# Second feed-forward block with its normalised input stored in reverse token order and read backwards by TensorE

## The chip, the cores and the metric

One Trainium2 chip, one of its cores. The metric is the device time of one execution in microseconds; of several executions the median is given. Operands of the large products are float32r, TensorE's reduced-precision float32, in high and low parts.

## What is computed

A trunk of two layers on 512 tokens of width 1024. Each layer has a mixer block and then a SwiGLU feed-forward block of hidden width 2816, both on an RMS-normalised input and added to the residual. The change touches the feed-forward block of the second layer:

```python
def rmsnorm(x, g):
    y = x * lax.rsqrt(jnp.mean(x * x, axis=-1, keepdims=True) + EPS)
    return y * g

for layer in range(2):
    x = x + mixer(layer, rmsnorm(x, mix_norm[layer]))     # two kinds of mixers
    h = rmsnorm(x, ffn_norm[layer])
    gate, up = jnp.split(h @ w_ffn_in[layer], 2, axis=-1)
    x = x + (jax.nn.silu(gate) * up) @ w_ffn_out[layer]
```

## The kernel before

**Layout.** The residual is held transposed, `xT`: 128 partitions (features), 8 feature tiles, 512 tokens along each partition. The input of each block is `xT` times the norm's gain; the factor of each token (`row_scale`, from the sum of squares) is applied after the projection. That input is kept in two parts of float32r, `h_hi` (ScalarE, `h_high`, L727: a copy that rounds to float32r) and `h_lo` (VectorE, `h_low`, L1146: xT times gain minus h_hi). There are four such rounds: `rnd` 0 and 2 before the mixers, 1 and 3 before the feed-forward blocks. Tiles are [128, 8, 512], so one feature tile of one part is 2 KB of consecutive memory in a partition.

**Products.** `product` (L1683 to L1685) makes three matmuls for each product of a weight tile and an input tile: high by high, high by low, low by high. The weights are the stationary operand (128 x 128), the 512 tokens the moving one, a PSUM bank of 512 float32 the result. The profile's names give the moving operand first in these groups: `ps<-h_hi,w_hi`.

**Weights.** The queue of SyncE brings 188 loads of up to 128 x 1024 float32 into two raw slots; ScalarE makes `w_hi` (L697), VectorE `w_lo` (L1122), in a ring of four slots. A slot is free when TensorE has read it (`load_used`). The order of all this is written out by hand in each engine's program; the steps of the feed-forward blocks are in a loop of five turns with two groups each.

**The second block's input projection** (`ffn_in(1, 0)`, rnd = 3) has 11 groups of 256 hidden columns, gate and up. A group takes 4 loads (`half_group`), each with 4 feature tiles and 2 banks. The first two loads of a group use the feature tiles 0 to 3, the other two 4 to 7. So the first group can start when the first four feature tiles of h are there, while VectorE still adds the second half of the mixer's output to `xT`. Between its second and third load stands the `mean` (L1716), a matmul of the matrix of ones with the sums of squares `acc`. ScalarE and VectorE make `row_scale` from it (L746, L751, L1181, L1187). Each group's result is taken out of PSUM by VectorE (L1406 gate times row_scale, L1410 up times silu), with ScalarE (L883 silu, L886 high part) and GpSimd (L581) between.

VectorE's order around the start of the block: `add_x` adds four banks to `xT` (L1382), and between these the operations of h_lo (L1146) and of the sum of squares (L1157, L1160) of the tile before; ScalarE makes h_hi (L727) and the squares (L735) as each `xT` tile comes.

The mixers, the first block and the output projections read h, where they do, with the same helper `H`, in token order.

Of the kernel before, what the change touches and what calls it, by code (L numbers as in the profile page):

```python
# [16 lines left out]
F32 = mybir.dt.float32  # L17
# [3 lines left out]
ACT = mybir.ActivationFunctionType  # L21
# [91 lines left out]
def program(nc, x, mix_norm, ffn_norm, w_ffn_in, w_ffn_out, e_w_in, e_conv, e_q_gain, e_k_gain,  # L113
# [11 lines left out]
    def sb(name, shape, dt=F32, size=4):  # L125
        n = size
        for d in shape[1:]:
            n *= d
        t = at(name, shape, dt, place[0])
        place[0] += (n + 63) // 64 * 64  # L130
        return t


    xT = sb("xT", [P, DT, S])
    h_at = place[0]
    h_hi = sb("h_hi", [P, DT, S], F32R)
    h_lo = sb("h_lo", [P, DT, S], F32R)
# [84 lines left out]
    ps = ctx.enter_context(nc.psum_tensor("ps", [P, 8, S], F32))  # L222

    def sem(name):
        return ctx.enter_context(nc.semaphore(name))
# [26 lines left out]
    h_hi_ready = sem("h_hi_ready")  # L252
# [278 lines left out]
    def g_col(i, a=0, b=P):  # L531
        return gains[a:b, i:i + 1]
# [117 lines left out]
    def h_gain(rnd, ft):  # L650
        return mix0_gain[:, ft:ft + 1] if rnd == 0 else g_col({1: G_FFN0, 2: G_MIX1, 3: G_FFN1}[rnd] + ft)

    X_BANKS = (4, 5, 6, 7, 4, 5, 6, 7)
    V_BANKS = ((0, 2), (3, 3))

# [21 lines left out]
    def _(act):  # L677
# [41 lines left out]
        def h_high_first(ft):  # L719

            act.wait_ge(x_turned, ft + 1)
            act.activation(h_hi[:, ft, :], ps[:, X_BANKS[ft], :], ACT.Copy, scale=h_gain(0, ft)).then_inc(h_hi_ready, 1)

        def h_high(rnd, ft):

            act.wait_ge(x_ready, 8 * rnd + ft + 1)
            act.activation(h_hi[:, ft, :], xT[:, ft, :], ACT.Copy, scale=h_gain(rnd, ft)).then_inc(h_hi_ready, 1)  # L727

        def h_square(rnd, ft):
            f = 8 * rnd + ft  # L730
# [6 lines left out]
        def fin(rnd, ft):  # L737
            h_high(rnd, ft)
            h_square(rnd, ft)
# [371 lines left out]
    def _(dve):  # L1111
        TT, STT, TS, TC = dve.tensor_tensor, dve.scalar_tensor_tensor, dve.tensor_scalar, dve.tensor_copy
# [25 lines left out]
        def fin(rnd, ft):  # L1138

            h_low(rnd, ft)  # L1140
            h_sum(rnd, ft)

        def h_low(rnd, ft):
            f = 8 * rnd + ft
            dve.wait_ge(h_hi_ready, f + 1)
            STT(out=h_lo[:, ft, :], in0=xT[:, ft, :] if rnd else ps[:, X_BANKS[ft], :], scalar=h_gain(rnd, ft), in1=h_hi[:, ft, :].bitcast(F32),  # L1146
                op0=ALU.mult, op1=ALU.subtract).then_inc(h_lo_ready, 1)

        def h_sum(rnd, ft):
# [63 lines left out]
        def x_copy(ft):  # L1213
            dve.wait_ge(x_turned, ft + 1)
            TC(xT[:, ft, :], ps[:, X_BANKS[ft], :]).then_inc(x_ready, 1)

        for ft in range(0, DT, 2):
            h_low(0, ft)
            if ft == 0:
                dve.wait_ge(first_high, 1)  # L1220
                low_slice(E_Q, 0).then_inc(first_low, 1)
            h_low(0, ft + 1)
            if ft == 0:
                dve.wait_ge(hi_done, E_Q + 1)
                low_slice(E_Q, 1).then_inc(lo_done, 1)
                nxt[0] = 1
            x_copy(ft)
            x_copy(ft + 1)
            through(-3 + ft // 2)
            h_sum(0, ft)  # L1230
            h_sum(0, ft + 1)
# [320 lines left out]
        for j in range(4):  # L1552
            STT(out=yc[:, j, :].rearrange("p (n i) -> p n i", n=QT), in0=ps[:, j, :].rearrange("p (n i) -> p n i", n=QT),
                scalar=g_col(G_V + j), in1=gate_bias[:, j:j + 1, :].broadcast_to([P, QT, P]),
# [123 lines left out]
    def _(pe):  # L1678
        MM = pe.matmul

        def product(dst, st_hi, st_lo, mv_hi, mv_lo, start, stop):

            MM(dst, st_hi, mv_hi, start=start, stop=False)  # L1683
            MM(dst, st_hi, mv_lo, start=False, stop=False)  # L1684
            return MM(dst, st_lo, mv_hi, start=False, stop=stop)  # L1685

        def ready(n, shift=0):
            pe.wait_ge(lo_done, n + 1 + shift)

        def load(n, tiles, ks, moving, banks, first, last, shift=0, extra=None, before=None):  # L1690

            ready(n, shift)
            hi_, lo_ = w_hi[:, n % W_SLOTS, :], w_lo[:, n % W_SLOTS, :]
            for kk, k in enumerate(ks):
                if kk and extra:
                    extra()
                mh, ml = moving(k)
                th, tl = tiles(hi_, kk), tiles(lo_, kk)  # L1700
                for t, b in enumerate(banks):
                    if before:
                        before(kk, t)
                    ins = product(ps[0:P, b, :], th[t], tl[t], mh, ml,
                                  first and kk == 0, last and kk == len(ks) - 1)
            ins.then_inc(load_used, 1)

        def plain(cols, count):

            return lambda w, kk: [w[:, cols * kk + P * t:cols * kk + P * t + P] for t in range(count)]  # L1710

        H = lambda k: (h_hi[:, k, :], h_lo[:, k, :])

        def mean(m, bank, weights, src):

            MM(ps[:, bank, :], weights, src, start=True, stop=True).then_inc(sums_ready, 1)  # L1716
# [25 lines left out]
        def turn_x(quarter):  # L1742

            pe.wait_ge(x_loaded[quarter], 16)
            for ft in (2 * quarter, 2 * quarter + 1):
                if ft >= 4:
                    pe.wait_ge(x_ready, ft - 3)
                for t in range(QT):
                    ins = pe.transpose(ps[:, X_BANKS[ft], t * P:(t + 1) * P], x_tok[:, t, ft * P:(ft + 1) * P], ident)
                ins.then_inc(x_turned, 1)  # L1750
# [36 lines left out]
        for ft, arrived in ((0, x_first), (1, x_loaded[0])):  # L1787
            pe.wait_ge(arrived, 16)
            for t in range(QT):
                ins = pe.transpose(ps[:, X_BANKS[ft], t * P:(t + 1) * P], x_tok[:, t, ft * P:(ft + 1) * P], ident)  # L1790
            ins.then_inc(x_turned, 1)
# [145 lines left out]
        def ffn_in(layer, bank0):  # L1937

            n0, n1, c = FFN_IN[layer], FFN_OUT[layer], 22 * layer
            rnd = 1 + 2 * layer  # L1940

            def half_group(n, j, b0, shift):

                load(n + j, plain(256, 2), range(4 * (j // 2), 4 * (j // 2) + 4), H,
                     (b0 + 2 * (j % 2), b0 + 2 * (j % 2) + 1), j < 2, j >= 2, shift)

            pe.wait_ge(x_ready, 8 * rnd + 4)
            for j in range(4):
                if j in (0, 2):
                    pe.wait_ge(h_lo_ready, 8 * rnd + 2 * j + 4)  # L1950
                half_group(n0, j, 4 * bank0, 0)
                if j == 1:
                    pe.wait_ge(x_ready, 8 * rnd + 8)
                    pe.wait_ge(h_summed, 8 * rnd + 8)
                    mean(M_FFN0 if layer == 0 else M_FFN1, (1 - bank0) * 4, ones, acc[:, :])
            pe.wait_ge(rs_step, (M_FFN0 if layer == 0 else M_FFN1) + 1)
            with pe.Fori(0, NG_FF // 2) as i:
                for g in (1, 2):

                    pe.wait_ge(hidden_ready, 1 + c + 2 * (g - 1) + 4 * i)  # L1960
                    for j in range(4):
                        half_group(n0 + 4 * g, j, 4 * ((bank0 + g) % 2), 8 * i)
# [67 lines left out]
        for j in range(4):  # L2030
            n = O_CV + j
# [293 lines left out]
```

## Time and profile before

| | |
|---|---|
| median of 3 timed runs | 1114.03 us (1114.01 to 1114.13) |
| span of the profiled execution, first to last instruction | 1112.0 us |
| mean granted TensorE clock | 1.000 |
| TensorE busy (matmuls) | 1102.9 us, 5105 instructions |
| VectorE, ScalarE, GpSimd busy | 560.2, 420.4, 102.9 us |
| first matmul of the second block's input projection | 748.99 us |
| first matmul of its output projection | 989.26 us |

The profile has the span of one execution; the timed runs are whole executions, about 2 us longer. Busy time of TensorE (PE) contains matmuls that overlap each other, so the distance between starts says more than the duration of one. PEld are the loads of the stationary operand. An instruction of plain float32 matmul is two records in the trace.

### The profile page before, as it was taken

What the parts mean: (1) busy time and instruction counts of PE and PEld (TensorE: products, weight loads), DVE (VectorE), ACT (ScalarE), POOL (GpSimd) and SP (SyncE); (2) the same over time, 40 slices, a digit from 0 to 9 for tenths busy, and PEclk for the clock granted to TensorE, in tenths of its full rate; (3) what the DMA queues carried; (4) which work ended last, traced back from release to release, by engine and by line L of the source; (5) the groups of instructions that cost most, each with busy time, mean ns of one, the idle gap of its engine ahead of it and who ended that gap; (6) DMA issues with size and microseconds to landing.
All of it is one profiled execution on the core that took longest, in us unless ns stands there. A gap on an engine that the chain in (4) does not pass through costs nothing. (4 is left out here: it accounts for less than half of the span.)

```text
span 1112.0 us, 13661 instructions
## 1 busy us (share of the span) xinstructions
PE 1102.9 (99%) x5105; PEld 887.1 (80%) x5105; DVE 560.2 (50%) x784; ACT 420.4 (38%) x662; POOL 102.9 (9%) x126
## 2 busy tenths in 40 slices
PE   8999999999999999999999999999999999999998
PEld 7777788888888888888877766788888888888887
DVE  6678977434433433242466588656433433453321
ACT  5545445333322322231345567544322322332110
POOL 6000000001000100000002023000000100110000
PEclk9999999999999999999999999999999999999999
DMA  7422223333333233322233200223233333327431
GB/s 236 159 57 76 76 75 96 114 95 95 94 94 94 94 102 103 98 95 85 67 103 94 77 35 1 77 96 112 89 101 94 94 97 100 102 78 170 113 123 48
DMA packets 101289, 106.00 MB, mean 95 GB/s; under 512 B 26235, under 2 KB 77888, under 8 KB 101120
## 3 DMA queue, kind: packets, MB, share of 16 engines
q1 hardware_dynamic: 83536, 103.04, 29.8%
q10 hardware_dynamic: 16656, 2.10, 1.1%
q8 instruction: 27, 0.44, 0.2%
q0 software_dynamic: 1056, 0.30, 0.1%
q14 instruction: 14, 0.11, 0.0%
HBM read 101.23 MB, written 2.10 MB: 93 GB/s over the span
## 5 line engine op out<-in xcount | busy, mean ns | idle before, releaser
L1122 DVE TENSOR_TENSOR w_lo<-raw,w_hi 128x1024 fp32r<-128x1024 f32 (+2 forms) x192 | 224.6, 1176 | 419.1 <-ACT w_hi L697 416.3
L697 ACT ACTIVATE w_hi<-raw 128x1024 fp32r<-128x1024 f32 (+2 forms) x192 | 194.2, 1017 | 468.7 <-PE ps L1685 438.4
L1683 PE MATMUL ps<-h_hi,w_hi 128*128 128x512 f32 x912 | 359.7, 394 | 1.0 <-DVE h_lo L1146 1.0
L1685 PE MATMUL ps<-h_hi,w_lo 128*128 128x512 f32 x912 | 355.1, 389 | 0.0
L1684 PE MATMUL ps<-h_lo,w_hi 128*128 128x512 f32 x912 | 355.0, 389 | 0.0
L1683 PEld LDWEIGHTS ps<-h_hi,w_hi 128*128 128x128 f32 x912 | 171.3, 188 | 42.9 <-issue 6.7
L1684 PEld LDWEIGHTS ps<-h_lo,w_hi 128*128 128x128 f32 x912 | 171.2, 188 | 36.7 <-issue 1.7
L1685 PEld LDWEIGHTS ps<-h_hi,w_lo 128*128 128x128 f32 x912 | 171.2, 188 | 35.9
L581 POOL TENSOR_TENSOR ffn_t<-ffn_t,row_scale 128x512 f32<-128x512 f32 x40 | 51.0, 1295 | 614.2 <-ACT ffn_t L883 614.2
L1684 PE MATMUL ps<-w_lo,act_hi 128*128 128x512 f32 (+1 forms) x178 | 68.8, 387 | 0.0
L1685 PE MATMUL ps<-w_hi,act_lo 128*128 128x512 f32 (+1 forms) x178 | 68.8, 387 | 0.0
L1683 PE MATMUL ps<-w_hi,act_hi 128*128 128x512 f32 (+1 forms) x178 | 68.8, 387 | 0.0
L1683 PE MATMUL ps<-act_hi,w_hi 128*128 (+1 forms) x176 | 68.5, 389 | 0.0
L1684 PE MATMUL ps<-act_lo,w_hi 128*128 (+1 forms) x176 | 68.5, 389 | 0.0
L1685 PE MATMUL ps<-act_hi,w_lo 128*128 (+1 forms) x176 | 68.5, 389 | 0.0
L1410 DVE TENSOR_TENSOR ffn_t<-ps,ffn_t 128x512 f32<-128x512 f32 x44 | 30.4, 692 | 44.8 <-POOL ffn_t L581 40.7
L886 ACT ACTIVATE act_hi<-ffn_t 128x512 f32 (+1 forms) x44 | 27.8, 633 | 49.3 <-DVE ffn_t L1410 49.3
L883 ACT ACTIVATE ffn_t<-ffn_t 128x512 f32<-128x512 f32 x44 | 27.1, 632 | 39.0 <-DVE ffn_t L1406 39.0
L1683 PEld LDWEIGHTS ps<-w_hi,act_hi 128*128 128x128 f32 x178 | 33.4, 188 | 6.9
L1684 PEld LDWEIGHTS ps<-w_lo,act_hi 128*128 128x128 f32 x178 | 33.4, 188 | 6.8
L1685 PEld LDWEIGHTS ps<-w_hi,act_lo 128*128 128x128 f32 x178 | 33.4, 188 | 6.7
L1683 PEld LDWEIGHTS ps<-act_hi,w_hi 128*128 128x128 f32 x176 | 33.0, 188 | 6.9
(283 smaller groups left out, 1173.4 us busy)
## 6 DMA issues: line engine op xcount, KB each, us to landing
raw<-in_w_ffn_in SPq DMA_DIRECT2D x88, 512.0 KB, 3.5
raw<-in_w_ffn_out SPq DMA_DIRECT2D x44, 512.0 KB, 3.7
raw<-in_e_w_in SPq DMA_DIRECT2D x17, 512.0 KB, 3.7
raw<-in_o_w_in SPq DMA_DIRECT2D x8, 512.0 KB, 3.6
raw<-in_o_w_out SPq DMA_DIRECT2D x8, 512.0 KB, 3.6
raw<-in_e_w_out SPq DMA_DIRECT2D x8, 256.0 KB, 3.9
raw<-in_e_w_out SPq DMA_DIRECT2D x4, 512.0 KB, 4.5
out_tok<-x_blocks ACTq DMA_DIRECT2D x16, 128.0 KB, 2.5
```

Of the source, the lines that this page charges most:

```text
L581: pool.tensor_tensor(ffn_t[:, t, :], ffn_t[:, t, :], row_scale[:, :], ALU.mult).then_inc(silu_scaled, 1)
L697: ins = act.activation(dst, src, ACT.Copy)
L883: act.activation(ffn_t[:, b, :], ffn_t[:, b, :], ACT.Silu).then_inc(silu_done, 1)
L886: act.activation(dst[:, t, :], ffn_t[:, (t0 + t) % 4, :], ACT.Copy).then_inc(hidden_hi, 1)
L1122: ins = TT(dst, src, high, ALU.subtract)
L1410: TT(ffn_t[:, b, :], ps[:, b0 + 2 + t, :], ffn_t[:, b, :], ALU.mult).then_inc(hidden_ready, 1)
L1683: MM(dst, st_hi, mv_hi, start=start, stop=False)
L1684: MM(dst, st_hi, mv_lo, start=False, stop=False)
L1685: return MM(dst, st_lo, mv_hi, start=False, stop=stop)
```

## The change

In round 3, and only there, h_hi and h_lo are written through a view with the token axis reversed, and all that reads them uses the same view: VectorE, which subtracts h_hi, and TensorE, whose moving operand starts at the last address of the 2 KB and goes down by one element a column. The columns come out in token order.

```diff
+    def h_order(tile, rnd, ft):
+
+        return tile[:, ft, ::-1] if rnd == 3 else tile[:, ft, :]
+
...
         def h_high(rnd, ft):
 
             act.wait_ge(x_ready, 8 * rnd + ft + 1)
-            act.activation(h_hi[:, ft, :], xT[:, ft, :], ACT.Copy, scale=h_gain(rnd, ft)).then_inc(h_hi_ready, 1)
+            act.activation(h_order(h_hi, rnd, ft), xT[:, ft, :], ACT.Copy, scale=h_gain(rnd, ft)).then_inc(h_hi_ready, 1)
...
             dve.wait_ge(h_hi_ready, f + 1)
-            STT(out=h_lo[:, ft, :], in0=xT[:, ft, :] if rnd else ps[:, X_BANKS[ft], :], scalar=h_gain(rnd, ft), in1=h_hi[:, ft, :].bitcast(F32),
+            STT(out=h_order(h_lo, rnd, ft), in0=xT[:, ft, :] if rnd else ps[:, X_BANKS[ft], :], scalar=h_gain(rnd, ft),
+                in1=h_order(h_hi, rnd, ft).bitcast(F32),
                 op0=ALU.mult, op1=ALU.subtract).then_inc(h_lo_ready, 1)
...
             def half_group(n, j, b0, shift):
 
-                load(n + j, plain(256, 2), range(4 * (j // 2), 4 * (j // 2) + 4), H,
+                load(n + j, plain(256, 2), range(4 * (j // 2), 4 * (j // 2) + 4),
+                     lambda k: (h_order(h_hi, rnd, k), h_order(h_lo, rnd, k)),
                      (b0 + 2 * (j % 2), b0 + 2 * (j % 2) + 1), j < 2, j >= 2, shift)
```

## Rows read from the trace of the kernel before

**Rows 1.** The page: span, busy time, TensorE's slices and granted clock.

```profile
span 1112.0 us, 13661 instructions
...
PE 1102.9 (99%) x5105; PEld 887.1 (80%) x5105; DVE 560.2 (50%) x784; ACT 420.4 (38%) x662; POOL 102.9 (9%) x126
...
PE   8999999999999999999999999999999999999998
...
PEclk9999999999999999999999999999999999999999
```

**Rows 2.** Windows: busy us (instructions) of PE, PEld, DVE, ACT, POOL; clock; DMA.

```profile
745.00:775.00 30.00, 30.00 (x132) 24.48 (x131) 19.69 (x27) 15.22 (x21) 0.00 (x0) 1.00 0.28 88
...
185.36:424.80 239.44, 239.44 (x1056) 197.91 (x1055) 100.68 (x118) 77.80 (x95) 25.47 (x20) 1.00 0.31 97
```

**Rows 3.** Timeline of TensorE, both ends of the second block's input projection: start, us.

```profile
748.99 0.39 PE L1683 MATMUL ps<-h_hi,w_hi 128*128 128x512 f32 x1
...
759.87 1.02 PE L1716 MATMUL ps<-acc,small 128*128 128x512 f32 x2
760.33 0.80 PE L1683 MATMUL ps<-h_hi,w_hi 128*128 128x512 f32 x1
...
989.03 0.39 PE L1685 MATMUL ps<-h_hi,w_lo 128*128 128x512 f32 x1
989.26 0.39 PE L1683 MATMUL ps<-w_hi,act_hi 128*128 128x512 f32 x1
```

**Rows 4.** The chain that ended last, around the mean: start, us, what.

```profile
760.03 0.86 PE ps L1716 x2
760.89 0.23 PE ps L1683
```

**Rows 5.** Waits from 757 to 992 us: us in total, times, longest.

```profile
ACT w_hi L697 <- PE ps L1685: 119.5, 33, 4.5
DVE w_lo L1122 <- ACT w_hi L697: 113.9, 34, 4.3
```

**Rows 6.** Timeline of TensorE, first and last of 21 matmuls of 256 columns.

```profile
655.55 0.28 PE L1683 MATMUL ps<-w_hi,ckv_hi 128*128 128x256 f32 x1
...
657.95 0.28 PE L1685 MATMUL ps<-w_hi,ckv_lo 128*128 128x256 f32 x1
```

**Rows 7.** Tile h_hi from 749 us on: ns min/median/max, first and last start.

```profile
L1683 PE MATMUL ps<-h_hi,w_hi x352: 387/389/799, 749.0 to 988.6; 128*128 128x512 f32 x176
L1685 PEld LDWEIGHTS ps<-h_hi,w_lo x352: 187/188/188, 749.2 to 988.8; 128*128 128x128 f32 x176
...
L727 ACT ACTIVATE h_hi<-xT,gains x4: 710/723/727, 752.1 to 756.8; 128x512 fp32r<-128x512 f32 x4
L1146 DVE SCALAR_TENSOR_TENSOR h_lo<-xT,gains,h_hi x4: 744/746/753, 752.9 to 757.9; 128x512 fp32r<-128x512 f32 x4
```

**Rows 8.** Timeline of VectorE around the start of the stage.

```profile
746.41 0.74 DVE L1146 SCALAR_TENSOR_TENSOR h_lo<-xT,gains,h_hi 128x512 fp32r<-128x512 f32 x1
...
751.43 1.28 DVE L1382 TENSOR_TENSOR xT<-ps,xT 128x512 f32<-128x512 f32 x2
...
757.90 0.75 DVE L1146 SCALAR_TENSOR_TENSOR h_lo<-xT,gains,h_hi 128x512 fp32r<-128x512 f32 x1
758.56 0.69 DVE L1160 TENSOR_TENSOR acc<-acc,sq 128x512 f32<-128x512 f32 x1
...
763.19 0.69 DVE L1187 SCALAR_TENSOR_TENSOR row_scale<-rs,y 128x512 f32<-128x512 f32 x1
...
774.09 1.28 DVE L1406 TENSOR_TENSOR ffn_t<-ps,row_scale 128x512 f32<-128x512 f32 x2
```

## The prediction

> **What bounds the kernel now.** I read the page first, then the work by stage, then the order of single matmuls at both ends of the second feed-forward block, and last the two engines that prepare its input.
>
> The page gives TensorE 1102.9 of 1112.0 us busy, and its slices are at nine tenths nearly everywhere, with the granted clock at full speed throughout [rows 1]. Busy TensorE alone proves little, since a matmul's 389 ns overlap the next one's. So look at the pace. In the first feed-forward block's input projection a window of 239.44 us holds 1056 matmul starts and 239.44 us of busy TensorE [rows 2]: one starts every 239.44 / 1056 = 0.2267 us. The second block's projection is the same work: 11 groups, 4 weight loads each, 4 slices of the contraction, 2 banks, 3 products: 11 x 4 x 4 x 2 x 3 = 1056. Its first matmul starts at 748.99, the next stage's first at 989.26 [rows 3]: 240.27 us. One float32 mean in between takes 0.86 us of the chain [rows 4], and 239.4 is left: again 0.2267 each. In the list of waits of this stage TensorE's matmuls don't stand at all; ScalarE waits 119.5 us for TensorE (the weights' slots) and VectorE 113.9 us for ScalarE [rows 5]. So this stage is TensorE's stream of matmuls and nothing else, 240 of 1112 us or 22%. Whatever each of its 1056 matmuls gains or loses comes out at the end in full; whatever the other engines lose is free up to their idle time.
>
> How far is the pace from the pure column rate? Products of 256 columns start every (657.95 - 655.55) / 20 = 0.120 us [rows 6], of 512 columns every 0.2267. The difference, 0.1067 us for 256 columns, is 2.4 columns per ns: the clock's upper level, one float32r column per cycle. The rest, 0.2267 - 0.2133 = 0.0133 us, is a fixed part for each matmul.
>
> **The change, part by part.** No instruction is added or removed and no wait is moved. Loads, slots, banks and semaphore counts stay. Three things get another address order.
>
> (a) The 8 ScalarE writes of h_hi (L727, 0.72 us each) store column 511 first [rows 7]. The input is still read forward. (b) The 8 VectorE operations that make h_lo (L1146, 0.75 us) read h_hi and write h_lo with a step of minus one [rows 7]; xT is read forward. (c) The 1056 moving operands are read from the last address down, so the columns arrive in token order; PSUM is written forward, the stationary side (the weights) is untouched, and nothing after the stage sees a difference. Two of three matmuls read h_hi, one reads h_lo.
>
> Parts (a) and (b): no row has such an order on either engine. A float32 operation of 512 columns at 0.72 to 0.75 us moves about 0.7 columns per ns, a third of what TensorE's reads make from the same memory, so I take nothing for them. From below: a gain has no mechanism, they touch the same 2 KB per partition. From above: let each take twice its time. First half of the tokens' features: the last h_lo ends at 746.41 + 0.74 = 747.15 and TensorE first reads at 748.99, so 1.8 us cover [rows 3, 8]. Four h_lo more (3.0) and one h_hi ahead of them (0.7) make 3.7, which is 1.9 too late. Second half: VectorE works without a gap from 751.43 to the last sum at 758.56 + 0.69 = 759.25, and the mean that needs it starts at 759.87: 0.6 us cover, so 3.7 becomes 3.1 too late [rows 3, 8]. Both in full: 5.0 us. Behind the mean the row scale is ready at 763.88 and first used at 774.09 [rows 8], 10 us of cover, so nothing grows further. GpSimd, 0.00 us busy from 745 to 775, isn't in the way of the two-source reads [rows 2].
>
> Part (c): this is the question. Bounds for one matmul: below, no change, since 2.4 columns per ns is already the clock's column rate and an order of addresses can't exceed it. The remaining 0.0133 us x 1056 = 14.1 us would be the most it could save, and I see nothing in the order that would remove it. Above, three rows. The fixed part doubled: 14.1 us. The pace of plain float32, where an instruction of 512 columns takes 0.86 / 2 = 0.43 us [rows 4]: 1056 x (0.43 - 0.2267) = 214.7 us. No overlap with the matmul before, 0.389 - 0.2267 = 0.162 us each [rows 7]: 171 us. I take no change: the row nearest in kind is the forward float32r read itself, which has the same width, the same number of columns and the same bytes; only the sign differs.
>
> The Trainium skill bears on the read (Advanced Engine Details and Errata, SBUF Cachelines): lines of 16 bytes, full performance while subsequent accesses hit the same line, and at least two hits on a line are needed to hide the memory's latency. A step of minus one float32 makes four hits on each line, as a step of plus one does, 128 lines for 512 columns either way; by that rule the sum stays at nothing. The rule says nothing of direction, and no row of this trace has a descending read, so it isn't tested here.
>
> Sum: 0 (a) + 0 (b) + 0 (c). The profiled execution spans 1112.0 us [rows 1]; the median of the timed runs is 1114.03, 2.0 above it, and that difference stays. Forecast 1114.0 us.
>
> **The rivals.**
>
> Half rate (the other side, slower). TensorE's reader may fetch float32r columns two at a time or ahead only in ascending order, and serve one column every other cycle otherwise. For it: the engine does have a slower way to stream 4-byte columns, 0.43 us for 512 [rows 4], and the forward stream is exactly at one column per cycle, with no reserve to lose. Against it: the slow float32 row is explained by the type alone, its operands are ascending too. It decides as soon as one matmul takes over 0.2267 us. Place: all 1056; price 214.7 us; time 1114.0 + 214.7 = 1328.7, the stage's share then 455 us. Clock unchanged, ScalarE and VectorE waiting longer for TensorE.
>
> A fixed price for each matmul. The first line of a descending read may be fetched later, without slowing the columns. The nearest row is the fixed part that is there already, 13.3 ns; once more, 14.1 us, time 1128.1. Against it: the weight load of 188 ns [rows 7] leaves 39 ns within each 227, so a few ns of start-up may also vanish there.
>
> Slow writes. ScalarE or VectorE at half pace in (a) and (b), at most 5.0 us, time at most 1119.0. For it: the second half has only 0.6 us of cover. Against it: only 16 instructions, and they run far below the reader's rate that TensorE shows.
>
> The change does nothing in the chip. The two reversals cancel in what is computed; if each pattern were turned back into an ascending one on the way to the chip, nothing could change. The time is the forecast's, 1114.0, so the time can't tell these two apart.
>
> **How the numbers follow.** A measurement of this kernel tells about 0.2% (2.2 us) from no change; the shown runs lie within 0.12 us. Chances: no change, by whichever way, 0.73; a fixed price per matmul 0.09; half rate 0.14; slow writes 0.03, of which a third stays under 2.2 us; a gain 0.01. Faster 0.01; same 0.73 + 0.01 = 0.74; slower 0.09 + 0.14 + 0.02 = 0.25. The range goes from 1112.5, a little under the runs, to 1130, the fixed price doubled with 2 us to spare; it holds 0.73 + 0.09 + 0.03 = 0.85 and leaves out half rate, which would stand alone far above. The likeliest case's own range is 1113 to 1116.
>
> **What would show it right or wrong.** In the changed kernel's profile: from the first to the last matmul of the second block's input projection 240.3 us, a start every 0.2267 us as in the first block, which is untouched and stands beside it as a reference; a matmul's own duration at 389 ns; ScalarE's h_hi at 0.72 and VectorE's h_lo at 0.75 us in that round as in the rounds before; the mean between the loads starting within 1.1 us of the matmul ahead. Half rate would show as about 0.43 us between starts and durations near 0.6; a fixed price as some 0.24 us; slow writes as long h_lo and a gap of TensorE near 749 or 760. What would make the forecast wrong is a reader that treats descending addresses in another way than ascending ones, which nothing in this trace can exclude.

## The result and the profile after

The changed kernel takes 1121.1 us (1120.73 to 1121.31) against 1114.03 before: a ratio of 1.0063 with a 95% interval of 1.0043 to 1.0083, some 7 us slower, a small difference but clear of the noise. The forecast of no change was wrong. The profiled execution spans 1119.3 us, 7.3 more than [rows 1].

The page of the changed kernel, its head, busy time and granted clock:

```profile
span 1119.3 us, 13661 instructions
...
PE 1110.2 (99%) x5105; PEld 887.6 (79%) x5105; DVE 560.2 (50%) x784; ACT 420.3 (38%) x662; POOL 103.1 (9%) x126
...
PEclk9999999999999999999999999999999999999999
```

The same instructions, the same clock, VectorE, ScalarE and GpSimd within 0.2 us of before; only TensorE is busy 7.3 us longer. The windows say where. The first row is the first block's input projection, the window of [rows 2]; the second lies within the second block's:

```profile
185.36:424.80 239.44, 239.44 (x1056) 197.90 (x1055) 100.69 (x119) 77.80 (x95) 25.45 (x20) 1.00 0.32 98
...
800.00:940.00 140.00, 140.00 (x602) 1.00 0.30 92
```

and the second window in the kernel before:

```profile
800.00:940.00 140.00, 140.00 (x619) 1.00 0.31 96
```

A window also counts the matmul cut by its left edge, so the time between starts is (window + one duration) / count: before (140 + 0.39) / 619 = 0.2268 us, after (140 + 0.40) / 602 = 0.2332. One matmul more or less in such a count is 0.0004 us. The untouched first block is at 0.2267 in both kernels. The timeline of TensorE at both ends of the changed stage, and the tile h_hi there (ns min/median/max, first and last start):

```profile
749.28 0.40 PE L1688 MATMUL ps<-h_hi,w_hi 128*128 128x512 f32 x1
...
760.49 1.02 PE L1721 MATMUL ps<-acc,small 128*128 128x512 f32 x2
760.94 0.80 PE L1688 MATMUL ps<-h_hi,w_hi 128*128 128x512 f32 x1
...
996.54 0.40 PE L1688 MATMUL ps<-w_hi,act_hi 128*128 128x512 f32 x1
```

```profile
L1690 PE MATMUL ps<-h_hi,w_lo x352: 395/397/398, 749.8 to 996.3; 128*128 128x512 f32 x176
L731 ACT ACTIVATE h_hi<-xT,gains x8: 707/722/725, 741.6 to 757.0; 128x512 fp32r<-128x512 f32 x8
L1150 DVE SCALAR_TENSOR_TENSOR h_lo<-xT,gains,h_hi x8: 745/748/753, 742.3 to 758.2; 128x512 fp32r<-128x512 f32 x8
```

The stage takes 996.54 - 749.28 = 247.26 us instead of the 240.27 of [rows 3]: 6.99 us more, or 0.0066 for each of 1056 matmuls. A matmul's own duration went from 389 ns [rows 7] to 397. The reversed writes of ScalarE and VectorE took 722 and 748 ns, against 723 and 746 [rows 7]: nothing. The mean starts 0.24 us behind the matmul ahead, as the matmuls around it do, so there is no gap. The other 0.3 us of the span is there before either block begins: TensorE's first matmul of the first block starts at 183.09 us, in the kernel before at 182.82. So the whole loss of the stage is a price for each matmul, of about 6.7 ns by the windows. That is 16 columns' time at the clock's upper level, 2.4 columns per ns.

### The profile page after: what moved, and what is told of

Same layout as the page of the kernel before. It is cut to its first block and busy times, and to the rows that moved or that the text cites. A ratio compares the mean times of both kernels' runs of the same rounds, so it can differ in the third digit from the quotient of the medians.

```text
span 1119.3 us, 13661 instructions
## 1 busy us (share of the span) xinstructions
PE 1110.2 (99%) x5105; PEld 887.6 (79%) x5105; DVE 560.2 (50%) x784; ACT 420.3 (38%) x662; POOL 103.1 (9%) x126
## 3 DMA queue, kind: packets, MB, share of 16 engines
q0 software_dynamic: 1056, 0.30, 0.1%
```

## The experiments

The first four ask what about the read is paid for, the next five whether it is the negative step, the last eight whether it is a price of the step at all. The edits are made in the changed kernel, but for one run that is made from the kernel before: most change `h_order` or the placement of tiles, three the size of the matmuls (384 columns, 256 columns, 64 stationary columns). Most runs are a single execution each, so what they tell is read from windows and timelines of the trace. Where one run holds two variants, the first block has one and the second the other, so that they stand in one trace.

### Both blocks backward

```diff
-        return tile[:, ft, ::-1] if rnd == 3 else tile[:, ft, :]
+        return tile[:, ft, ::-1] if rnd in (1, 3) else tile[:, ft, :]
```

> The first feed-forward block's input projection reads backwards too, so 2112 matmuls descend. Theory A (each descending float32r read of 512 columns takes 6.7 ns more, 0.2334 instead of 0.2267 us between starts): the first block's projection grows by 1056 x 0.0067 = 7.0 us as the second did, total 1114.0 + 14.1 = 1128.1 us. Rival (the 7 us of the changed kernel belong to something of the second block only, for instance where its memory lies or what runs beside it): the first block stays at 0.2267 us, total about 1121.

Measured 1128.13 us (1127.86 to 1128.58), 1.0123 times before (1.0106 to 1.014). Windows within the first and the second block's projection:

```profile
260.00:380.00 120.00, 120.00 (x516) 1.00 0.31 96
...
800.00:940.00 140.00, 140.00 (x602) 1.00 0.30 94
```

The first block now has (120 + 0.40) / 516 = 0.2333 us too. The price goes with the reads, some 14 us for 2112, as theory A has it, and has nothing to do with the second block's place in the program.

### Only the low part backward

```diff
+        return tile[:, ft, ::-1] if rnd == 3 and tile is h_lo else tile[:, ft, :]
```

> Only h_lo of the second block is stored in reverse and read with a step of minus one; h_hi is as before. In each product of three matmuls one descends and two ascend. Theory A (a price for each descending read): 352 x 6.7 ns = 2.3 us, three matmuls take 0.6867 us instead of 0.6800, span near 1114.4. Rival (a price for each change of direction between neighbouring reads): two changes in each product, 704 x 6.7 = 4.7 us, 0.693 us for three. Rival (the price falls on all once any read descends): 7.0 us. If it is a price for a stream that never ascends: nothing.

Measured 1116.14 us in one run, span 1114.3; the window from 800 to 940:

```profile
800.00:940.00 140.00, 140.00 (x613) 1.00 0.31 94
```

(140 + 0.39) / 613 = 0.2290 us a matmul, 0.687 for three: one price in three. It isn't a price of changing direction, and it needs no run of backward reads.

### 384 columns

```diff
+                    if cut and not (first and kk == 0):
+                        ins = product(ps[0:P, b, 0:384], th[t], tl[t], mh[:, 0:384], ml[:, 0:384], False, last and kk == len(ks) - 1)
+                        continue
```

> In both blocks' input projections all matmuls but those of the first feature tile of each group read and write 384 columns instead of 512 (the last 128 tokens lack 7 of 8 feature tiles in these sums); the first block ascends, the second descends. Before: 0.0133 + 384 / 2.4 = 0.1733 us between starts ascending. Theory A1 (6.7 ns fixed for each read): descending 0.1800. Theory A2 (a price for each column or line, 0.013 ns a column): descending 0.1783.

66 matmuls of 384 columns in a row of the first block, and 66 of the second; first and last of each:

```profile
295.83 0.33 PE L1688 MATMUL ps<-h_hi,w_hi 128*128 128x384 f32 x1
...
307.11 0.33 PE L1690 MATMUL ps<-h_hi,w_lo 128*128 128x384 f32 x1
...
852.56 0.34 PE L1688 MATMUL ps<-h_hi,w_hi 128*128 128x384 f32 x1
...
864.11 0.34 PE L1690 MATMUL ps<-h_hi,w_lo 128*128 128x384 f32 x1
```

Forward 11.28 / 65 = 0.1735, backward 11.55 / 65 = 0.1777: 4.2 ns more, not 6.7. Theory A1, the fixed price (0.1800), already fails here; A2, a price by the column (0.1783), comes nearer. (The expectation for 256 columns further down takes this run for a fixed price, which it isn't.) The whole execution took 1024.32 us.

### Blocks in reverse, or reversed blocks

```diff
+        if rnd == 1:
+            return tile[:, ft, :].rearrange("p (b c) -> p b c", b=8)[:, ::-1, :]
+        return tile[:, ft, :].rearrange("p (b c) -> p b c", b=8)[:, :, ::-1] if rnd == 3 else tile[:, ft, :]
```

> Two parts of the reversal by themselves. In the first block the 512 tokens are stored as 8 blocks of 64 in reverse order of the blocks, and read by a two-level pattern: outer step minus 64, inner step plus one. In the second block each block of 64 is stored in reverse inside, and read with outer step plus 64, inner step minus one. Theory A (what costs is the inner step of minus one, once for a read): first block 0.2267 us, second 0.2334. Rival (each jump against the ascending order restarts the reader, some 6.7 ns each): 7 to 8 jumps in both, 0.27 to 0.28 us in both. Rival (only the start at the tile's upper end costs): first block starts at element 448, second at element 63, so both pay about the same.

Measured 1121.53 us, one run. Windows:

```profile
260.00:380.00 120.00, 120.00 (x531) 1.00 0.32 100
...
800.00:940.00 140.00, 140.00 (x601) 1.00 0.30 93
```

531 in 120 us is what the kernel before has, 0.2267: seven jumps backward and a start at element 448 cost nothing. The inner step of minus one costs 0.0067, the same with eight reversed blocks as with one reversed row. So jumps and the start at the tile's end are out. All runs with 512 columns up to here fit a price of the negative inner step (theory A); the run with 384 says that it isn't fixed.

### 256 columns

The edit is that of the run with 384, with 256.

> As the run with 384 columns, with 256: all matmuls but those of each group's first feature tile read and write 256 columns (the last 256 tokens lack 7 of 8 feature tiles in these sums); first block ascending, second descending. Before, 256 ascending columns take 0.120 us. Theory A1 (a fixed 16 cycles of 2.4 GHz = 6.7 ns for each descending read, as 384 and 512 columns showed): 0.1267. Rival (with short reads the load of the stationary operand sets the pace, and the 6.7 ns hide behind it): 0.120.

35 matmuls of the first block and 52 of the second, first and last of each:

```profile
297.83 0.28 PE L1688 MATMUL ps<-h_hi,w_hi 128*128 128x256 f32 x1
...
301.91 0.28 PE L1689 MATMUL ps<-h_lo,w_hi 128*128 128x256 f32 x1
...
828.88 0.28 PE L1689 MATMUL ps<-h_lo,w_hi 128*128 128x256 f32 x1
...
834.91 0.28 PE L1689 MATMUL ps<-h_lo,w_hi 128*128 128x256 f32 x1
```

Forward 4.08 / 34 = 0.1200, backward 6.03 / 51 = 0.1182. Theory A fails here: with 256 columns the backward read isn't dearer but slightly cheaper. So the difference is 6.7 ns at 512 columns, 4.2 at 384 and -1.8 at 256, neither fixed nor in proportion to the columns. The granted clock was 1.00 in both stretches (0.98 over the whole execution of 981.32 us, in which TensorE also has gaps).

### Forward from moved places, backward from moved places

```diff
+    place[0] += 64
+    h_wide = at("h_wide", [P, 2 * DT * S + 16], F32R, h_at)
...
+        first = (1 if rnd == 1 else 15) + (4096 if tile is h_lo else 0) + 512 * ft
+        return h_wide[:, first:first + 512]
```

(The backward run has 1 and 8 elements, and `[:, ::-1]`.) The 64 bytes of room put the raw slots, the weights and the small tables behind them 64 bytes higher as well, which turned out to matter more than what was meant to be tried.

> No step of minus one anywhere: both blocks read forward, but h lies 4 bytes higher in the first block's projection (each read starts at the second float32 of a 16-byte line and touches one line more) and 60 bytes higher in the second's (it starts at the last float32 of 64 bytes). Theory A (the price is for a negative inner step): 0.2267 us in both. Rival B (the price is for where a read starts within a line or a 64-byte piece, a descending read starting at its last element): 0.2334 in the second block, perhaps in both.

> Both blocks read backwards, 2112 descending reads; h lies 4 bytes higher in the first block (a read starts at the first float32 of a line) and 32 bytes higher in the second (in the middle of 64 bytes). Theory A (a fixed price for the negative step, wherever it starts): 0.2334 us in both, span near 1126. Rival B (the price depends on where the descending read starts, for instance the reader has to take the whole of a piece first): other paces in the two, one of them 0.2267.

1140.6 and 1140.67 us, one run each, both far above the changed kernel. Windows of the forward run: first block's input projection (h 4 bytes higher), its output projection (act where it was), second block's input projection (h 60 bytes higher); then the backward run's two input projections:

```profile
260.00:380.00 120.00, 120.00 (x501) 1.00 0.30 92
470.00:540.00 70.00, 70.00 (x302) 1.00 0.29 91
800.00:940.00 140.00, 140.00 (x615) 1.00 0.31 96
```

```profile
260.00:380.00 120.00, 120.00 (x511) 1.00 0.30 91
...
800.00:940.00 140.00, 140.00 (x602) 1.00 0.31 94
```

Forward reads without any negative step take 0.2403, 0.2331 and 0.2283 us. So forward reads pay as well, up to twice the price of the reversal (13.6 ns). The output projection is the telling one: its moving tiles didn't move, only its weights did. Backward reads take 0.2356 and 0.2332. The two first blocks differ in the direction alone: h 4 bytes and the weights 64 bytes higher, 0.2403 forward (501 matmuls) and 0.2356 backward (511). In this place the backward read is 4.7 ns cheaper than the forward one, so the price of the reversal changes even its sign with the place. Theory A and theory B are both too simple; I formed theory D, that the place of the moving read and that of the stationary tile's load count together.

### Steps of two and four

```diff
+    h_two = at("h_two", [P, DT, S, 2], F32R, h_at)
+    h_four = at("h_four", [P, DT // 2, S, 4], F32R, h_at)
...
+        if rnd == 1:
+            return h_two[:, ft, :, part]
+        return h_two[:, ft, ::-1, part] if rnd == 3 else tile[:, ft, :]
```

> h_hi and h_lo of both feed-forward blocks lie interleaved, element by element, so a read has step plus two in the first block and minus two in the second (two elements of each 16-byte line). Theory A (a negative inner step costs 6.7 ns a read, a positive one nothing): 0.2267 and 0.2334 us. Rival C (any inner step other than plus one costs): 0.2334 or more in both. If the number of lines counts, both are well longer than 0.2334, by the same per column.

> As the run with steps of two, but four vectors lie interleaved (high and low part of two feature tiles), so a read has step plus four in the first block and minus four in the second: each column is in another 16-byte line. The Trainium skill's page Advanced Engine Details and Errata, SBUF Cachelines, says that less than two hits on a line cost time. Worked out from rows: if a column then takes two cycles, 0.0133 + 512 / 1.2 = 0.44 us between starts in the first block, 0.447 in the second, total 1114 + 2 x 225 = 1565 us. Theory A with no price for lines: 0.2267 and 0.2334 us, total 1121.

1604.62 and 1623.3 us. The run with steps of two, first block (+2) and second (-2):

```profile
260.00:380.00 120.00, 120.00 (x268) 1.00 0.15 48
...
1250.00:1350.00 100.00, 100.00 (x216) 1.00 0.15 45
```

With steps of four:

```profile
260.00:380.00 120.00, 120.00 (x262) 1.00 0.16 48
...
1250.00:1350.00 100.00, 100.00 (x212) 1.00 0.15 47
```

A matmul's own duration is 0.63 to 0.67 here, so +2 is (120 + 0.63) / 268 = 0.450 us, -2 is 0.466, +4 is 0.461, -4 is 0.475. That is about two cycles of 2.4 GHz a column already at a step of two. That is near the pace which the half-rate rival named; it comes with the size of the step, not with its sign. On top of it, a negative sign costs some 16 and 14 ns here, with about 2 ns of grain in such counts. The Trainium skill (Advanced Engine Details and Errata, SBUF Cachelines) says that at least two hits on a 16-byte line are needed to absorb the memory's latency, and that the tolerance of strides depends on the type. Read as two elements of each line being enough, that isn't so for float32r moving operands here: two of each line go at half rate, and one of each line costs only 11 ns more (0.461 against 0.450). The measurement decides.

### Weights 64, 128 and 256 bytes higher, h where it was

```diff
+    place[0] += 64
     w_hi = sb("w_hi", [P, W_SLOTS, 1024], F32R)
```

The small tables that lie behind the weights move with them; `row_scale`, `acc` and `act` start at the next multiple of 1024 bytes and stay.

> The changed kernel with w_hi and w_lo 64 bytes higher in each partition; h stays where it was, so the first block reads it forward as before, the second backwards. Theory D (the 6.7 ns are no price of the direction, but of where the moving read and the load of the next stationary tile stand to each other, as the forward reads of the run moved by 4 bytes and 60 bytes suggest, in which the weights lay 64 bytes higher too): the first block's forward reads now take 0.2333 us or more instead of 0.2267, and the second block's may take another time than 0.2334. Theory A (negative step alone): 0.2267 and 0.2334.

> The changed kernel with the weights 128 bytes higher. With 64 bytes forward reads took 0.2334 us, with 256 bytes 0.2267. If the relation of the two reads repeats every 128 bytes: 0.2267 forward and a total near 1121; if every 256: 0.229 or more forward, total 1130 to 1139. Backward 0.2333 either way, if it doesn't depend on the place.

> As the run with the weights 64 bytes higher, with 256 bytes. If the two reads meet modulo 64, 128 or 256 bytes, the forward pace is 0.2267 and the backward 0.2334 as in the changed kernel, total about 1121; if modulo more, 0.2333 forward, total about 1138.

1138.74, 1138.07 and 1120.7 us, one run each. Windows of the three, first block forward, second backward:

```profile
260.00:380.00 120.00, 120.00 (x516) 1.00 0.30 92
...
800.00:940.00 140.00, 140.00 (x601) 1.00 0.31 97
```

```profile
260.00:380.00 120.00, 120.00 (x518) 1.00 0.30 92
...
800.00:940.00 140.00, 140.00 (x601) 1.00 0.30 94
```

```profile
260.00:380.00 120.00, 120.00 (x531) 1.00 0.32 101
...
800.00:940.00 140.00, 140.00 (x602) 1.00 0.29 90
```

Forward reads: 0.2333, 0.2324, and with 256 bytes 0.2267 again. Of the three distances only 256 bytes gives the old pace. Backward reads: 0.2336, 0.2336, 0.2332, the same within the grain of such a count. As far as 0, 64, 128 and 256 bytes tell, the relation repeats after 256 bytes.

### Both operands 64 bytes higher

The edit is that of the moved reads, with 16 elements in both blocks and `[:, ::-1]` in the second.

> Weights 64 bytes higher and h of both feed-forward blocks 64 bytes higher too: the two operands stand to each other as in the kernel before, forward in the first block, backward in the second. Theory D (the relative place of the two reads counts): the first block's forward reads are back at 0.2267 us, while the output projection of the first block, whose act tiles stay and whose weights move, takes 0.2333; backward stays near 0.2334. Rival E (each operand's own alignment counts, a start that is no multiple of some larger size costs): 0.2333 or more forward.

1131.41 us, one run. Input projection of the first block, its output projection (weights moved, act not), input projection of the second, backward:

```profile
260.00:380.00 120.00, 120.00 (x531) 1.00 0.32 96
470.00:540.00 70.00, 70.00 (x301) 1.00 0.29 90
800.00:940.00 140.00, 140.00 (x602) 1.00 0.30 94
```

Moved together, forward reads are back at 531 in 120 us, 0.2267; the output projection, where only one of the two moved, stays at (70 + 0.40) / 301 = 0.2339. So it isn't either operand's own alignment, at 64 bytes: it is their places in relation to each other. That is theory D as far as forward reads go.

### Every read forward, weights 64 bytes higher

The edit of the run with 64 bytes, made in the kernel before.

> The kernel before, every read forward, with nothing changed but w_hi and w_lo 64 bytes higher. Theory D: 0.2333 us for forward reads of h and of act with the weights as stationary operand, 0.2289 where the weights are the moving one; total near 1138.7 as in the run with the weights moved and the second block backward, since backward added nothing there. If a backward read had its own price on top of the place, this kernel would be 7 us faster than that run, 1131.7.

1139.33 us (1138.43 to 1140.88), 1.0224 times before (1.0207 to 1.0241), against 1138.74 with the second block backward. In this place a backward read costs nothing more than a forward one, 602 matmuls here and 601 there:

```profile
260.00:380.00 120.00, 120.00 (x516) 1.00 0.30 92
...
800.00:940.00 140.00, 140.00 (x602) 1.00 0.31 97
1040.00:1090.00 50.00, 50.00 (x216) 1.00 0.44 119
```

The last row is the second block's output projection, where the weights are the moving operand; the run with the same placement and the second block backward has 220 there. The addresses of that stage are the same in both, the pace 0.2333 against 0.2290. So the pace hangs on something besides addresses, perhaps on how the stage was entered.

### Half as many stationary columns

```diff
+                    if cut and not (first and kk == 0) and not (last and kk == len(ks) - 1):
+                        ins = product(ps[0:64, b, :], th[t][:, 0:64], tl[t][:, 0:64], mh, ml, False, False)
+                        continue
```

> In both blocks' input projections the matmuls of 6 of the 8 feature tiles load and compute only 64 of the 128 stationary columns (the other 64 hidden columns of each tile lack these sums); forward in the first block, backward in the second, 512 columns moving. Theory D (the price comes from the load of the next stationary tile and the moving read meeting): with half the load the forward and the backward pace change, and their difference isn't 6.7 ns. Theory A (the negative step's own price): 0.2267 or a common lower value forward, exactly 6.7 ns more backward.

Windows, forward then backward:

```profile
260.00:380.00 120.00, 120.00 (x525) 1.00 0.31 96
...
800.00:940.00 140.00, 140.00 (x602) 1.00 0.30 94
```

The total was 1123.1 us. With half the stationary columns the forward pace got worse, 0.2293 over all tiles instead of 0.2267, and the backward one stayed at 0.2332. The difference of the two isn't a constant 6.7 ns. The run halves the load and the computed columns together, so it doesn't show which of the two the forward pace depends on; that it is the load is theory D's reading, and only argued.

### Each tile of h in another place

```diff
+        first = 512 * ft + OFFSETS[ft] + (4096 + 128 if tile is h_lo else 0)
+        moved = h_wide[:, first:first + 512]
+        return moved[:, ::-1] if rnd == 3 else moved
```

> Weights where they were. The 8 feature tiles of h (high and low part alike) lie 0, 4, 8, 16, 32, 48, 60 and 64 bytes past their old places, modulo 512; forward reads in the first block, backward ones in the second. Theory D: the pace of a tile depends on its offset, in both directions, in whole steps of about 6.7 ns, and some offset gives backward reads 0.2267. Theory A: 0.2267 at every offset forward, 0.2334 backward.

> As the run with small offsets, with 0, 96, 128, 192, 256, 320, 384 and 448 bytes. Theory D: a pattern that repeats with the size of what the two reads collide in (64, 128, 256 or 512 bytes). Theory A: 0.2267 forward, 0.2334 backward at all.

Here everything behind h, the weights too, lies 1024 bytes higher, which is the same place modulo 512.

1127.61 and 1127.69 us. Forward 521 and 519 in 120 us (0.2311, 0.2320), backward 596 and 600 in 140 (0.2356, 0.2340). Both directions lose in a mixed layout. Theory A had 0.2267 and 0.2334 at every offset, so it fails again; theory D's expectation that some offset gives backward reads 0.2267 isn't met in any window either. The pace of single tiles can't be given to one offset, since neighbouring matmuls had other offsets; I draw nothing more from them.

## Why the prediction was wrong

What bounds the kernel, and that the stage is TensorE's stream alone, held: 6.99 of the 7.3 us of span are in the stage, and a change of each matmul came out in full.

(a) and (b), the reversed writes and VectorE's reversed read at no cost, held: 722 and 748 ns. The slow-writes rival is out.

(c) failed, at one step: "I take no change: the row nearest in kind is the forward float32r read itself". The term of the sum that was put at nothing measured 0.2332 us a matmul instead of 0.2268, 6.99 us for the stage. The time of that row wasn't a property of forward reads. It was the best case of all forward reads measured, and it goes with the places in which weights and h stand to each other; the same forward read takes 0.2333 with the weights 64 bytes higher and 0.2403 with h 4 bytes and the weights 64 higher. The pace I had divided into 0.2133 for columns and 0.0133 fixed, and then treated the fixed part as a constant. It is the part that varies. "Only the sign differs" was true of the addresses, but took for granted that the pace doesn't depend on the order in which they come.

The fixed-price rival, at a chance of 0.09, came nearest, in form: a small price on each matmul instead of half the rate. Its size was mis-set, 13.3 ns by the row taken against 6.7 measured, so 1128.1 against 1121.1. Its reason, a first line fetched later "without slowing the columns", isn't borne out: such a price would be the same at 384 and 256 columns, and it was 4.2 and -1.8 ns. That 1121.1 us lies within the range of 1112.5 to 1130 is owed to the room left for this rival, not to the forecast's mechanism; the likeliest case's own range, 1113 to 1116, doesn't hold it. Half rate didn't come with the reversal; of the steps tried, two and four bring it. That the reversal might not reach the chip is out, since the pace changed.

The Trainium skill's rule on lines gave no change for a step of minus one, and the trace disagrees: 0.2332 instead of 0.2268, with four elements a line in both. The rule says nothing of the other operand's place, on which the forward pace hangs here.

**What is shown and what isn't.** Shown: the inner step of minus one costs 6.7 ns for each matmul of 512 columns in this layout, nothing in the layout with the weights 64 bytes higher, and less than nothing (-4.7 ns) with h 4 and the weights 64 bytes higher; forward reads have a better pace, 0.2267, that hangs on the relation of moving and stationary addresses; backward reads of 512 columns never got under 0.2332 in a window, in any of the places tried. Only argued: that the two reads of TensorE get into each other's way, and that a backward read can't keep the favourable relation with a stationary load that runs forward. A reversed stationary tile would be a test of that, and no run has one. Open: why the price falls with the columns, to 4.2 ns at 384 and to a gain of 1.8 ns at 256, and what beside addresses sets the pace of the second output projection.

## What to carry to other kernels

In a stream of short products bound by TensorE, compare the measured time between starts with columns over clock; the rest is not a constant, and both an inner step of minus one and a placement that differs by 64 bytes can change it by 3%. Before adding or removing a small tile ahead of weights or activations, look at that pace in the trace: here 64 bytes cost 25 us, the reversal 7. An order that can be made by jumps between blocks of 64 with a forward inner step was free here (eight blocks). Inner steps of two and four took twice the time of a float32r moving operand with a step of one, so such layouts are best undone before TensorE reads them.

## What the runs showed that was not expected

- Moving w_hi and w_lo by 64 bytes made the kernel before 2.2% slower (1139.33 against 1114.34 us in the same series), with every instruction and count the same.
- The kernel before had this relation right in the stages looked at (both feed-forward blocks): 0.2267 us.
- A float32r moving operand with step two takes 0.450 us for 512 columns, with step four 0.461, with step one 0.2267.
- An outer step of minus 64 with an inner step of one costs nothing: 0.2267 us.
- With h 4 bytes and the weights 64 bytes higher, the backward read is the faster one: 0.2356 us against 0.2403 forward.
